# Choosing keys beside a projection, and turning an attention's output inside the projection behind it

## What is computed

```python
aq, ak, av, iq, ik, iw, bq, bk, bv = jnp.split(h @ w_in, cuts, axis=-1)
...
out_a = dsa_attention(aq, ak, av, iq, ik, iw, t5_bias[:, :A_HEADS_2])
...
lam = (jnp.exp(jnp.sum(lq1.astype(jnp.float32) * lk1.astype(jnp.float32)))
       - jnp.exp(jnp.sum(lq2.astype(jnp.float32) * lk2.astype(jnp.float32))) + lambda_init)
out_b = diff_attention(bq, bk, bv, lam, b_subln, t5_bias[:, A_HEADS_2:]) * (1.0 - lambda_init)
return jnp.concatenate([out_a, out_b], axis=-1) @ w_out
```

## Time and profile before

| | us |
|---|---|
| median of 3 runs | 1747.04 (1746.64 to 1747.14) |
| the profiled execution, its own time | 1735.48 |
| its span on the engines | 1733.9 |
| TensorE busy | 1653.0 (95%) |
| VectorE busy | 1066.8 (62%) |
| ScalarE busy | 853.1 (49%) |
| mean granted TensorE clock | 0.969 |

### The profile page before, as it was taken

The page is one execution under the profiler, slowest core; times in us unless marked ns, Lnnn a source line. Parts: engine busy times, 40 slices in busy tenths (PEclk is TensorE's granted clock), DMA queues, the critical chain, the costliest instruction groups (busy, mean ns, idle before and its releaser), DMA issues.

```text
span 1733.9 us, 25053 instructions
## 1 busy us (share of the span) xinstructions
PE 1653.0 (95%) x10412; PEld 1486.4 (86%) x10412; DVE 1066.8 (62%) x1545; ACT 853.1 (49%) x1223; POOL 23.6 (1%) x26
## 2 busy tenths in 40 slices
PE   7988988999999999997989999999999999999998
PEld 7876877899989998885777999889998878789997
DVE  5555658688756564676757665455554766766553
ACT  4454645666545443553446544354443555664442
POOL 0000002000000000000000000000000000000000
PEclk9988989999999999997689999999999999999999
DMA  7747223555554555442033554545554542525553
GB/s 272 275 146 245 101 98 146 190 187 180 187 191 163 179 190 193 177 172 95 1 131 137 194 189 176 194 173 191 173 192 170 194 146 74 190 102 187 178 194 122
DMA packets 42976, 290.21 MB, mean 167 GB/s; under 512 B 5048, under 2 KB 5198, under 8 KB 9968
## 3 DMA queue, kind: packets, MB, share of 16 engines
q1 hardware_dynamic: 38272, 271.93, 43.8%
q0 software_dynamic: 4592, 16.69, 2.8%
HBM read 287.51 MB, written 8.55 MB: 171 GB/s over the span
## 4 chain that ended last, share of the span: by engine, by line
PE 88%; DVE 5%; DMA 2%; ACT 2%; issue 1%; DVEq 1%; SPq 0%; POOL 0%; ACTq 0%
PE bank L454 26%; PE bank L455 26%; PE bank L456 26%; PE bank L460 7%; DMA raw<-stream_dram 2%; PE bank L724 2%; DVE low L422 1%; PE bank L1504 1%; PE bank L606 1%; DVEq L2414 1%; ACT high L411 1%; PE bank L1702 0%; DVE u L983 0%; DVE h L1109 0%; DVE u L659 0%
## 5 line engine op out<-in xcount | busy, mean ns | idle before, releaser
L411 ACT ACTIVATE high<-raw 128x2048 fp32r<-128x2048 f32 x257 | 488.9, 1914 | 535.4 <-DMA raw<-stream_dram 525.7
L422 DVE TENSOR_TENSOR low<-raw,high 128x2048 fp32r<-128x2048 f32 x255 | 582.8, 2293 | 248.1 <-ACT high L411 246.9
L454 PE MATMUL bank<-xh,high 128*128 128x256 f32 x1880 | 535.1, 285 | 1.1 <-DVE low L422 1.1
L455 PE MATMUL bank<-xl,high 128*128 128x256 f32 x1880 | 533.5, 284 | 0.0
L456 PE MATMUL bank<-xh,low 128*128 128x256 f32 x1880 | 533.5, 284 | 0.0
L454 PEld LDWEIGHTS bank<-xh,high 128*128 128x128 f32 x1880 | 362.3, 193 | 2.1 <-issue 1.5
L455 PEld LDWEIGHTS bank<-xl,high 128*128 128x128 f32 x1880 | 362.3, 193 | 0.0
L456 PEld LDWEIGHTS bank<-xh,low 128*128 128x128 f32 x1880 | 362.2, 193 | 0.0
L454 PE MATMUL bank<-high,xh 128*128 128x512 f32 (+2 forms) x528 | 206.7, 391 | 5.6 <-DVEq L2414 3.2
L456 PE MATMUL bank<-high,xl 128*128 128x512 f32 (+2 forms) x528 | 203.6, 386 | 0.0
L455 PE MATMUL bank<-low,xh 128*128 128x512 f32 (+2 forms) x528 | 203.5, 385 | 0.0
(11 more groups left out here) (229 smaller groups left out, 1555.9 us busy)
## 6 DMA issues: line engine op xcount, KB each, us to landing
raw<-stream_dram SPq DMA_DIRECT2D x257, 1024.0 KB, 4.8
band_wide_dram<-band_rows_dram POOLq DMA_DIRECT2D x1, 3072.0 KB, 30.9
t_wide_dram<-t_rows_dram POOLq DMA_DIRECT2D x1, 2304.0 KB, 15.1
u<-mem_dram POOLq DMA_DIRECT2D x2, 1024.0 KB, 5.2
bias<-band_wide_dram POOLq DMA_DIRECT2D x1, 2048.0 KB, 15.3
rel_wide_dram<-rel_rows_dram POOLq DMA_DIRECT2D x1, 1920.0 KB, 15.7
bias<-t_wide_dram POOLq DMA_DIRECT2D x1, 1536.0 KB, 8.2
bias<-rel_wide_dram POOLq DMA_DIRECT2D x1, 1280.0 KB, 7.0
```

What stands on the lines that cost most here:

```text
L411: act.activation(self.high[:, n % RING, :], self.raw[:, n % RING, :], ACT.Copy).then_inc(self.high_split, 1)
L422: dve.tensor_tensor(self.low[:, n % RING, :], self.raw[:, n % RING, :], self.high[:, n % RING, :].bitcast(F32), ALU.subtract).then_inc(sel ...
L454: pe.matmul(out, lh, rh, start=start, stop=False)
L455: pe.matmul(out, lh, rl, start=False, stop=False)
```

## The change

- The columns of the weight matrix are put in another order: the indexer's queries come in job 1, so that they are turned by the end of job 2.
- `Select` and `Lambda` are no longer stages. `Project` calls `select.tensor`, `select.scalar` and `select.vector` in its jobs. The units are done two to a job from job 3 on, block 1 first; TensorE scores them behind tiles 2 and 5 of the job. VectorE sums them behind its two splits and ahead of the job's drain, then does the search parts that `PARTS` names: block 1 in jobs 4, 5 and 6, all of block 0 in job 7. Lambda comes in job 6.
- The turned rows of the projection have two banks instead of four (`ring=2`), the scores have banks 6 and 7.
- `Attention` has no search any more and gets `fill=16`.
- The `Turn` stage goes. `TurnedResidual` turns attention A's half (no norm) ahead of the first matmul, and attention B's normed half behind the twelve matmuls of tile 0.

```diff
-    main = r(0, 512) + r(512, 512) + r(1536, 512) + r(2120, 512) + r(2632, 512) + r(1024, 512) + r(3144, 512)
+    main = r(1536, 512) + r(0, 512) + r(512, 512) + r(2120, 512) + r(2632, 512) + r(1024, 512) + r(3144, 512)
```

```diff
     def bank(self, g):
-        return self.core.bank[self.base + g % 4]
+        return self.core.bank[self.base + g % self.ring]
```

```diff
-        self.turn = Turn(core, batches or [None] * len(jobs), base=4)
+        self.turn = Turn(core, batches or [None] * len(jobs), base=4, ring=2 if select else 4)
...
                 else:
                     c.release(last, m, i0 + j)
+                if self.select:
+                    self.select.tensor(pe, s, n, j)
             if n and self.turn.batches[n - 1][1]:
...
             c.split_high(act, m.slot(i0 + len(kts) - 1))
+            if self.select:
+                self.select.scalar(act, s, n)
             c.wait_output(act, m, i0 + len(kts) - 1, s, self.others[n])
...
             c.split_low(dve, m.slot(i0 + len(kts) - 1))
+            if self.select:
+                self.select.vector(dve, s, step, n)
             c.wait_output(dve, m, i0 + len(kts) - 1, s, self.others[n])
```

```diff
+
+class TurnedResidual(Residual):
+
+
+
+    def __init__(self, core, name, x, kts, turn, **options):
+        super().__init__(core, name, x, kts, **options)
+        self.turn = turn
+
+    def input_wait(self, pe, s, k):
+        if k == 0:
+            self.turn.turn_rows(pe, s, 0)
+        pe.wait_ge(s["turned_by_dve"], NB if k < self.kts // 2 else 2 * NB)
+        if k == 1:
+            self.turn.turn_rows(pe, s, 1)
+
+    def scalar(self, act, s):
+        self.turn.copy_high(act, s, 0)
+        self.turn.square_rows(act, s, 1)
+        self.core.split_high(act, self.m.first)
+        self.turn.copy_high(act, s, 1)
+        super().scalar(act, s)
+
+    def vector(self, dve, s):
+        self.turn.copy_low(dve, s, 0)
+        self.turn.scale_rows(dve, s, 1, Steps(dve, s["dve_step"]))
+        self.core.split_low(dve, self.m.first)
+        self.turn.copy_low(dve, s, 1)
+        super().vector(dve, s)
```

```diff
+class Select:
+
+
+
+    FIRST = 3
+    UNITS = [(b, pair) for b in (1, 0) for pair in ((0, 2), (1, 3), (4, 6), (5, 7))]
+    TILES = (2, 5)
+    PARTS = {4: (4,), 5: (5,), 6: (6, 7), 7: (0, 1, 2, 3)}
+    LAMBDA = 6
...
+    def positive(self, i):
+        return self.core.square[:, i % 2, HALF:D].rearrange("p (j k) -> p j k", j=2)
+
+    def of_job(self, n):
+        first = 2 * (n - self.FIRST)
+        return [i for i in (first, first + 1) if 0 <= i < len(self.UNITS)]
+
+    def tensor(self, pe, s, n, k):
+        if not self.of_job(n) or k not in self.TILES:
+            return
+        c = self.core
+        i = self.of_job(n)[self.TILES.index(k)]
+        b, pair = self.UNITS[i]
+        nk = (b + 1) * P
+        if i == 0:
+            pe.wait_ge(s["turned_by_act"], 2)
+            pe.wait_ge(s["turned_by_dve"], 2)
+        if i >= 2:
+            pe.wait_ge(s["keys_positive"], i - 1)
+        for j, h in enumerate(pair):
+            last = mm(pe, c.bank[6 + i % 2][:, j * S:j * S + nk], self.q(h)[:, b * P:(b + 1) * P],
+                      self.k(h)[:, 0:nk], True, True)
+        last.then_inc(s["keys_scored"], 1)
+
+    def scalar(self, act, s, n):
+        c = self.core
+        for i in self.of_job(n):
+            b, pair = self.UNITS[i]
...
+            act.wait_ge(s["keys_scored"], i + 1)
             if i >= 2:
...
+                act.wait_ge(s["keys_summed"], i - 1)
+            ps = c.bank[6 + i % 2][:, :].rearrange("p (j k) -> p j k", j=2)[:, :, 0:nk]
+            act.activation(self.positive(i)[:, :, 0:nk], ps, ACT.Relu, scale=DH ** -0.5)\
+               .then_inc(s["keys_positive"], 1)
+        if n == self.LAMBDA:
+            act.wait_ge(s["lam_sums"], 1)
+            act.activation(c.small[:, 146:148], c.small[:, 144:146], ACT.Exp).then_inc(s["lam_exps"], 1)
+
+    def vector(self, dve, s, step, n):
+        if n == self.FIRST:
+            for b in range(NB):
+                step(dve.tensor_scalar(self.w[:, b, :], self.weights(b), 8 ** -0.5, None, ALU.mult))
+        if n == self.LAMBDA:
+            self.lam_sums(dve, s, step)
+        for i in self.of_job(n):
+            b, pair = self.UNITS[i]
+            nk = (b + 1) * P
+            dve.wait_ge(s["keys_positive"], i + 1)
             for j, h in enumerate(pair):
...
+            m.then_inc(s["keys_summed"], 1)
+            dve.wait_ge(s["keys_summed"], i + 1)
+        for part in self.PARTS.get(n, ()):
+            self.search(dve, step, part)
+        if n == self.LAMBDA:
+            self.lam(dve, s, step)
```

```diff
+def even_turn(c):
+
+
+    def groups(q, need, gain):
+        return [(need and need + b, [c.o[:, b, (q + j) * P:(q + j + 1) * P] for j in range(4)], P, "pair",
+                 (c.oh[:, q:q + 4, block_cut(b)], c.ol[:, q:q + 4, block_cut(b)]), gain) for b in range(NB)]
+
+    norms = [(c.o[:, b, HALF:D].rearrange("p (h d) -> p h d", d=P), 1.0 - LAMBDA_INIT) for b in range(NB)]
+    return Turn(c, [((), groups(0, 0, None)), (norms, groups(4, 1, PARAM(c.param, "subln")))])
```

```diff
+    at = [2 * HALF, 0] + [n * HALF for n in (1, 3, 4, 5, 6)]
     jobs = [(tail, 0, range(KT), 136, [u[:, b, 3584:3720] for b in range(NB)])]
-    jobs += [(m, n * KT, range(KT), HALF, [u[:, b, n * HALF:(n + 1) * HALF] for b in range(NB)]) for n in range(7)]
-    batches = [head_batch(c, 3584, P, 12, "idx_k"), head_batch(c, 0, HALF, 0, "a_q"), head_batch(c, HALF, HALF, 4, "a_k"),
-               head_batch(c, 2 * HALF, HALF, 8, None), head_batch(c, 3 * HALF, HALF, 13, "b_q"),
-               head_batch(c, 4 * HALF, HALF, 17, "b_k"), None, None]
+    jobs += [(m, n * KT, range(KT), HALF, [u[:, b, at[n]:at[n] + HALF] for b in range(NB)]) for n in range(7)]
+    batches = [head_batch(c, 3584, P, 12, "idx_k"), head_batch(c, 2 * HALF, HALF, 8, None),
+               head_batch(c, 0, HALF, 0, "a_q"), head_batch(c, HALF, HALF, 4, "a_k"),
+               head_batch(c, 3 * HALF, HALF, 13, "b_q"), head_batch(c, 4 * HALF, HALF, 17, "b_k"), None, None]
+    select = Select(c, lambda h: half(t[:, 8:12, :], h), lambda h: t[(h % 2) * DH:(h % 2 + 1) * DH, 12, :],
+                    lambda b: u[:, b, 3712:3720])
     st = [Project(c, x, jobs, source=Source(c, c.h, x, gain="l0_mix", norm=True), scale=True, batches=batches,
...
+                  masked=12, select=select)]
```

```diff
-    st.append(Attention(c, units, select))
-    norms = [(c.o[:, b, HALF:D].rearrange("p (h d) -> p h d", d=P), 1.0 - LAMBDA_INIT) for b in range(NB)]
-    st.append(out_turn(c, 8, PARAM(c.param, "subln"), norms))
+    st.append(Attention(c, units, fill=16))
...
-            st.append(Residual(c, "even_out", turned, KT, loads=Loads((c.u[:, :, 2048:3072], mem))))
+            st.append(TurnedResidual(c, "even_out", turned, KT, even_turn(c), loads=Loads((c.u[:, :, 2048:3072], mem))))
```

More of the change, by code:

```diff
@@ L1461, with __init__ @@
 class Attention(Stage):
-    def __init__(self, core, units, select=None, loads=None, fill=0):
+    def __init__(self, core, units, loads=None, fill=0):
         super().__init__(core)
-        self.fill = fill
-        self.units, self.select, self.loads = units, select, loads
+        self.units, self.loads, self.fill = units, loads, fill
     def gpsimd(self, pool, s):
@@ L1593, in vector @@
                 logits(i + 2)
-            if self.select and i < 8 and i % 2 == 0:
-                self.select.search(dve, step, 4 + i // 2)
             if i >= 2:
@@ L1665, with __init__ @@
     OUT_BANK = 4
-    def __init__(self, core, units, fill, select=None, loads=None):
-        super().__init__(core, units, select, loads)
+    def __init__(self, core, units, fill, loads=None):
+        super().__init__(core, units, loads)
         self.groups = fill
@@ L1799, in vector @@
                 logits(i + 3)
-            if self.select and i < 8:
-                self.select.search(dve, step, 4 + i // 2)
             if i:
@@ L2048, in __init__ @@
         self.score = c.xn[:, 1, 0:HALF].rearrange("p (b k) -> p b k", b=NB)
         self.best = c.xn[:, 1, HALF:HALF + 16].rearrange("p (b k) -> p b k", b=NB)
-        self.w = c.square[:, 2, 0:16].rearrange("p (b h) -> p b h", b=NB)
-        self.units = [(b, pair) for b in range(NB) for pair in ((0, 2), (1, 3), (4, 6), (5, 7))]
-    def tensor(self, pe, s):
-        c = self.core
-        for i, (b, pair) in enumerate(self.units):
+        self.w = c.square[:, 2, HALF:HALF + 16].rearrange("p (b h) -> p b h", b=NB)
@@ L2250, in memory_stages @@
     return out
-def out_turn(c, tiles, gain=None, segments=()):
-    groups = []
-    for b in range(NB):
-        for q in range(0, tiles, 4):
-            n = min(4, tiles - q)
-            cut = (slice(None), slice(q, q + n), block_cut(b))
-            groups.append((len(segments), [c.o[:, b, (q + j) * P:(q + j + 1) * P] for j in range(n)], P, "pair",
-                           (c.oh[cut], c.ol[cut]), gain if q >= 4 else None))
-    return Turn(c, [(list(segments), groups)])
```

(14 more changed lines are left out.)

74 lines of the change are left out of this document (21 added, 53 removed).

## The result

| | before | after |
|---|---|---|
| median of 4 runs each | 1746.84 us (1742.20 to 1747.14) | 1715.83 us (1712.50 to 1719.27) |
| ratio | | 0.9829 [0.9803, 0.9854] |
| the profiled execution | 1735.48 us | 1716.07 us |
| its span, mean clock | 1733.9 us, 0.969 | 1714.1 us, 0.983 |

31.0 us faster by the medians, 19.4 by the two profiled executions. The page of after, as the earlier trace rows: head, busy shares, granted clock in 40 slices.

The account below looks back on a forecast made before the run. TensorE, busy 95% of the span, was taken as the bound, its idle time before the even mixer's attention also lowering the clock. Gains 3.7 + 11.3 + 6.5 = 21.5 us off a 1747.0 median gave 1725.5 us, range 1717 to 1741.

Parts of the forecast that it names:

- The step that failed: Outside the traced stretch: the median's 11.6 us above the profiled execution was taken as unchanged by the change.
- the sum: Whole kernel: gains of 3.7 (projection), 11.3 (attention) and 6.5 (output), 21.5 us together, taken off the median.
- the very mechanism that the prediction describes: Even mixer: TensorE's idle time lowers the clock for what follows; dense fill matmuls bring it back within about 5 us.
- its rival of no change: Low clock holds to the attention's end, whose last 14.4 us grow by 8, eating the 8.0 gained: 1747; chance 0.04.
- The projection: Last matmul at 803.0, VectorE 7.2 us late, stage ends at 811.0 against 814.67: 3.7 us gained.
- The attention: Starts at 0.50, fill restores the clock; 40 us against 51.3, ending at 851: 11.3 us gained.
- row without fill: Attention: 37 busy microseconds at 0.50 in the profile before, by which without fill it keeps its 51 us.
- The output: From the attention's end into w_out: 11.4 us of gap and low clock become 4.9: 6.5 us gained.
- clock stays low: Rival in the attention: fill too short or cut by scores, attention runs as before, 8.0 us gained, 1739; chance 0.24.
- VectorE was not less late: Rival before the attention: VectorE less late, TensorE's idle time shrinks to 3 us, clock holds: 1717.5; chance 0.10.
- the projection did not starve: Rival "slower": VectorE's queue bounds the projection, 14.5 us lost, TensorE starves, low clock behind: 1753.5; chance 0.04.

Follow-up runs that it names:

- e1: The kernel before, unedited, run again: median 1741.66 us over 12 runs (1742.25 over 22 later runs).
- e11: e7 without the 16 fill matmuls behind the attention's first scores (fill=0), both other fills kept: 1721.85 us.
- e8: The changed kernel with one quarter instead of four of block 0's search, so block 0 keeps too many keys: 1705.50 us.
- e2: The changed kernel without the attention's 16 fill matmuls (fill=0): 1729.82 us, 0.9920 of before.
- e7: The changed kernel with the edits of both e5 and e6: 1708.13 us.
- e6: The changed kernel plus four bare matmuls in each attention step without scores and ten behind the output projection's first eight transposes: 1712.17 us.
- e9: The changed kernel, unedited, measured again as yardstick: 1714.04 us, 0.9842 of before.
- e3: The kernel before with only fill=16 added in the even mixer's attention: 1731.17 us, 0.9938 of before.
- e4: The changed kernel with the old separate output turn stage and Residual in place of TurnedResidual: 1718.82 us, 0.9869 of before.
- e5: The changed kernel plus 44 bare matmuls on TensorE behind the projection, after waiting for positive keys: 1709.45 us.
- e7b: The kernel of e7, unedited, measured again in the third group: 1711.61 us.
- e10: e7 with the second drains of jobs 6 and 7 on ScalarE in place of VectorE: 1705.37 us.

## Why the prediction was wrong, step by step

**The step that failed** is the last one of the sum: "11.6 more, of which the trace says nothing; I take it as unchanged". The changed kernel's profiled execution took 1716.07 us (1714.0 forecast) and its median is 1715.83: the 11.6 are gone. They were not a constant beside the kernel. The runs show two parts:

- *A longer low clock in the mixer, some 7 us.* In before, how long the clock stays at 0.50 differs from one execution to the next, and the execution that was profiled first was a lucky one, in which it came back 14.4 us ahead of the attention's end. In e1 it did not, and S is 7.4 us longer. That is about the distance from the first profiled execution to the median of 22 runs (1742.25 - 1735.48 = 6.8). This part the change removes: it is the very mechanism that the prediction describes. The prediction even had the price: in its rival of no change the low clock holds to the end and the last 14.4 us grow by 8; e1 shows it as 58.8 - 51.3 = 7.5 us. It was applied to the kernel after, not to the median before.
- *Three runs that were no fair sample, some 5 us.* They lay within 0.5 us of each other (1746.64 to 1747.14), and the prediction took the noise for 0.2%. Of the 22 later runs only four are above 1746.5 us, and they reach down to 1730.4. From 1742.25 the sum would have given 1720.8. What makes a run of 1747 us is not profiled. An estimate from the clocks: 0.960 over such a run's 1745.3 us is 140 us at 0.50, of which a mixer like e1's accounts for 85; the rest, 55, is near what the first block has in the profile with most of it (51 in e11).

**The projection** was right in its end and wrong within. A unit costs TensorE more than its own matmuls: the transposes of successive jobs stand 766.02 - 751.67 = 14.35 us apart with two units of 256 keys and 13.5 with two of 128, against 11.8 without, so 1.27 and 0.87 us a unit, not 1.05 and 0.55. That makes 8.6 for the eight, not 6.4. With it the last matmul ends at 805.0 and not 803.0. It did not count, since VectorE comes last anyway: 811.37 against 811.0. VectorE's last drain starts 5.4 us behind that matmul, not 7.2, but the end of its queue, added up piece by piece from groups and a timeline, was right within 0.4 us, and e8 confirms that this queue sets the start. TensorE waited for VectorE within no later job, as forecast.

**The attention** was right in its mechanism: low clock at its start (2.04 us for the scores, 2.0 forecast), fill 3.01 (3.5), back at 1.00 3.7 us after the start (within 5), end at 850.2 (851). The 38.9 us for 40 hold some luck. With no low clock at all it takes 35.2 us, fill included (e8, 807.55 to 842.74), where the forecast had 37 and put the fill on top; the slow start cost 1.7 more, and 1.9 went to a second fall of the clock, at 845.9, that the forecast did not have inside the attention. By the row without fill it would have kept the low clock, and e2's profile shows that: 71.6 us. The Trainium skill, "TensorE: Matmul & The Clock Gate", part on the clock gate, has activity release the low clock; e1's attention, with TensorE busy for 57.8 of 58.8 us and at 0.50 throughout, and e11, busy for 20.50 of 20.50 us at 0.50, are against reading "busy" in a profile as that activity. The same page warns that the records of the clock can be wrong. Here the durations bear them out: the twelve records of the first scores last 2.04 us at 0.50 (after) and 1.13 at 1.00 (e7), four of value products 1.22 (e1) and 0.71 (after).

**The output** was oversized: 3.9 us gained, 6.5 forecast. The pieces were right in kind (meeting 0.72; transposes to the first matmul 3.42, where 2.8 were forecast; no wait for the norms, where 0.5 was), but they ran at 0.50. The clock fell 4.3 us ahead of the attention's end, where I had put it possibly behind: the values took 3.51 us (1.96 in e8), the eight transposes 1.94 (1.06), and the first 12 matmuls of `w_out` ran at half speed. Forecast for a fall there were 1.5 us; S of e6, which removes it, is 3.9 shorter than in e9, part of it inside the attention.

**The rivals.** The clock did not stay low, VectorE was not less late, and the projection did not starve. With 24% on "clock stays low" the range went up to 1741 but ended 1.2 us above the time, because none of the cases let before's own median contain what the change removes, or be too high.

## What to carry to other kernels

If a profiled execution and the median lie apart, take more runs and compare their mean clocks before building a forecast on one profile; a change that removes a low-clock stretch takes away what that stretch costs in the median run, not only what it cost in the execution that happened to be profiled. Price such a stretch at its longest as well, as if the clock came back only behind the thin work. And where TensorE must wait some microseconds ahead of thin work, give it matmuls that nobody reads there and again behind the first scores: in this kernel each place was worth something that the other did not give.

## What the runs showed of the hardware

- One kernel without any edit took 1730.4 to 1747.7 us over 22 runs, in order of its mean clock to within 0.002 (0.972 to 0.960). The kernels with the 16 matmuls and no other edit on the clock (after, e9, e3, e4) spread by 4 to 7 us.
- TensorE stayed at 0.50 for 85.2 us in which it was busy for 69.2 (e1), and for 20.5 us in which it was busy for all 20.5 (e11). In the thin attention the clock came back on its own late or not at all (838.3 in e11, 851.6 in before, not in the profiles of e1 and e2). With the 16 dense matmuls it was back 1.6 to 2.1 us from their start in all five profiles that began them at 0.50 (after, e3, e4, e6, e9), with those of `w_out` in 3.1 us in before and 5.5 in e2. In e1, e3 and e4 it was back ahead of `w_out`, 4.3, 4.3 and 3.1 us from the start of the 16 transposes of the output.
- From 1.00, the same thin attention fell to 0.50 within 3.6 us of its start without the 16 matmuls (e11), and with them stayed at 1.00 throughout (e7).
- Around the attention's end the clock did not do the same in all profiles, though their attention has the same instructions there: it fell ahead of the end, for 13.7 us, in after and e9, behind it, for 6.8 us, in e4 and e5, not at all in e8. In the five profiles with bare matmuls there (e6, e7, e7b, e10, e11) it did not fall. What decides between them among the first five is open.
- A unit's products slipped in between dense fast matmuls cost TensorE 1.27 and 0.87 us, some 0.15 more than the 1.13 and 0.71 of their records.
